# Block 1 of a two-model kernel: decay rows by DMA instead of by matmul, and a new order of slabs around the state scan

## The chip, the core and the metric

One core of one Trainium2 chip. The time is device microseconds of one execution of the whole program, median of several runs. The kernel before took 2516.99 us (three runs, 2516.38 to 2517.11).

## The reference, cut to what matters

The program runs two layers of block 1 and two of block 2 on one sequence of 512 positions with 1024 features. Only block 1 is changed. In it, one normed input `h` is multiplied by one wide matrix, and the columns feed three branches:

```python
h = rmsnorm(x, attn_norm_g[layer])
gm_u, gm_v, ssm_z, ssm_xbc, ssm_dt, da_q, da_k, da_v, gates = split_cols(h @ w_in[layer], IN_SIZES)
y_a = gelu(gm_u) * (causal(w_s) @ rmsnorm(gelu(gm_v)) + b_s)          # in chunks of 128
# mamba2: 16 heads of 64, 2 groups, state 128, chunks of 128
xs, bm, cm = split(silu(conv(xbc)));  dt = softplus(ssm_dt + bias)
a_cum = cumsum(dt * a)                                               # per head, per chunk
decay = exp(where(causal, a_cum[t] - a_cum[s], -inf))                # the head's decay matrix
y = (C.B * decay) @ (xs*dt) + C @ prev_state * exp(a_cum) + d*xs
y_b = rmsnorm(y * silu(z))
y_c = diff_attention(q, k, v)
merged = g0*(y_a @ w_branch_a) + g1*(y_b @ w_branch_b) + g2*(y_c @ w_branch_c)
```

For each head the decay needs `a_cum` as a row (position t along the free axis) on all 128 partitions; that row is what the change obtains in another way.

## The kernel before, in words

**Weights and precision.** All large products are made of three fp32r matmuls (high by high, low by high, high by low; `mm3`, L571 to L573). A weight slab is 128 x 1024 words (512 KB), for branches a and c 128 x 512 (256 KB). Each slab goes through four steps: SP issues its load (`load`, L545) as soon as the slab four places earlier is done; ACT rounds it to `w_hi` (L561, `hi_ahead`); DVE subtracts to get `w_lo` in place (L566, `lo_ahead`); PE multiplies. ACT and DVE work three slabs ahead of PE (`LEAD = 3`, `RAW = HI = 4`). A slab of 512 KB is 24 matmuls of 512 columns, one of 256 KB is 12.

**Queues.** Every engine runs one program written out by hand, in order. What is queued behind a waiting instruction waits too. PE writes slabs into four PSUM banks (`pg`, `take_bank`) and everything else into four more in rotation (`pm`, `take_pm`): the i-th use of `pm` waits until the use four before it has been emptied. The order of the `pm` uses is the list `PM.take(...)`.

**The stage in question**, once for each of the two layers (at 107 to 300 us and at 1020 to 1213 us in the profile). PE's order before: 12 xbc slabs; 4 z slabs; transposes of dt and cumulative decays (`dt_n`), then 4 z slabs with two transposes of xs (`xs_n`) ahead of each; 4 gu slabs, each followed by transposes of B or by a C.B product; the spatial mixing (`gm_mix`); 8 gate_a slabs with the three chunk states between them; 8 branch-a slabs, and between them for each pair of heads p two fp32r matmuls that spread a row of `a_cum` over all partitions (`ac_rows`, L2244, from a hi/lo split `ac_parts`) and the 28 small fp32 matmuls of the pair (`y_pair`, L2269 and L2272); then 12 qkv slabs. Each qkv group of four slabs fills four banks, tile tt after tile tt; bank tt is taken at the first slab of the group.

**Around the pairs**, for head h of pair p: DVE takes the minimum of row and column (`bounded`, L1535, reading the row in PSUM), ACT makes the exponentials (L1019 over 384 columns, L1021 four times 128), POOL multiplies the first by C (L2074), and DVE (even head, L1574) or POOL (odd head, L2077) multiplies the second by C.B. DVE adds the pair's result to `yf` (L1570), and merges each branch-a unit with its gate (L1566), which frees the unit's bank. POOL also makes `yf = d*xs` (L2049, 8 times, "y_init") and the low parts `ya_lo` (L555).

Of the kernel before, what the change touches and what calls it, by code (L numbers as in the profile page):

```python
# [13 lines left out]
P = 128  # L14
# [99 lines left out]
def program(nc, t, out, depth=DEPTH, depth2=DEPTH):  # L114
    with ExitStack() as ctx:
# [53 lines left out]
        head_row = sb("head_row", [P, SSM_H], F32R)  # L169
# [80 lines left out]
        wt_gm = conv_in[:, 0, 4:4 + SEQ].rearrange("p (g n) -> p g n", g=GM_G)  # L250
# [6 lines left out]
        xw = [conv_in[:, 2 + g, 4:4 + SSM_I // SSM_G] for g in range(SSM_G)]  # L257
# [8 lines left out]
        ac_parts = over("ac_parts", arena_at + 4 * 26624, [P, SEQ], F32R)  # L266
# [51 lines left out]
        for name, slabs, units in [("gv", 4, 4), ("dt", 0, 1), ("xbc", 12, 12), ("z", 8, 8), ("gu", 4, 4), ("gate_a", 8, 8), ("a", 8, 8), ("qkv", 12, 12),  # L318
                                   ("gate_b", 8, 8), ("b", 8, 8), ("gate_c", 8, 8), ("c", 8, 8), ("out", 8, 8), ("up", 44, 44), ("down", 24, 8)]:
# [7 lines left out]
        for p in range(PAIRS + 1):  # L327
            if p < PAIRS:
                PM.take(("ac_row", p), 2)
            if p >= 1:  # L330
                PM.take(("y", p - 1), 1)
# [157 lines left out]
        def gate_unit(i):  # L489
# [10 lines left out]
                "gm_vn": TT, "decay_in": 1, "decays": 1, "dt_ready": TT, "ac_split": 1, "gm_wt_ready": 1, "ya_ready": GM_G, "ya_hi_done": GM_G,  # L500
                "ya_split": GM_G, "ac_zeroed": 1, "cb_masked": SSM_G, "seg_bound": SSM_H, "seg_exp": SSM_H, "y_init": KD, "c_exp": SSM_H, "c_scaled": SSM_H, "decay_cb_even": PAIRS, "decay_cb_odd": PAIRS, "y_sq": KD, "y_sq_added": KD - 1, "xw_ready": SSM_G * (TT - 1), "y_gated": KD, "y_rms": 1, "y_inv": 1,
                "yb_ready": KD, "yb_hi_done": 8, "yb_split": 8, "qk_ssq": TT, "qk_rms": 1, "qk_ready": 1, "lam_dot": 1, "lam_exp": 1,
                "neg_max": 2 * DA_H * TT, "w_ready": DA_H * TT, "sub_summed": 1, "sub_rms": 1, "yt_ready": DA_H, "gates_b": 1, "gate_a_last": 1, "b_merged": KD, "gates_c": 1,
# [362 lines left out]
        def _(act):  # L866
# [24 lines left out]
            act.wait_ge(setup, 8)  # L891
# [22 lines left out]
            for l in range(depth):  # L914
# [65 lines left out]
                hi_ahead(SL["z"] + 2)  # L980
                z_in(0)
                for j in range(3, 7):
                    hi_ahead(SL["z"] + j)
                z_in(1)
                act.wait_ge(S("decay_in"), past("decay_in") + 1)
                nc.scalar.activation(dts[:, 128:256], dts[:, 128:256], ACT.Exp).then_inc(S("decays"), 1)
                hi_ahead(SL["z"] + 7)
                pm_filled(act, PM["gm_wt"])
                nc.scalar.activation(wt_gm.rearrange("p g n -> p (g n)"), pmb(PM["gm_wt"]), ACT.Copy).then_inc(pm_free[PM["gm_wt"] % 4], 1)

# [5 lines left out]
                for g in range(GM_G):  # L996
                    bank = unit_filled(act, SL["gu"] + g, UN["gu"] + g)
                    nc.scalar.activation(ya[:, g, :], bank, ACT.Gelu_apprx_tanh).then_inc(bank_free[(UN["gu"] + g) % BANKS], 1)
                    left_of("b_n" if g < 2 else "cb", bn if g < 2 else cb, g % 2)
                    hi_ahead(SL["gu"] + g)  # L1000
# [5 lines left out]
                act.wait_ge(S("y_init"), past("y_init") + KD)  # L1006
                for i in range(KD - 1):
                    gates(m_val, SL["gate_a"], UN["gate_a"], i, 1, ACT.Sigmoid)
                    hi_ahead(SL["gate_a"] + i)

                act.wait_ge(pm_ready, PM[("state", TT - 2)] + SSM_G)
                for p in range(PAIRS):
                    if p >= 2:
                        act.wait_ge(pm_ready, PM[("y", p - 2)] + 1)
                    for h in (2 * p, 2 * p + 1):
                        u = PM[("ac_row", p)] + h % 2
                        bank = pm_filled(act, u)
                        act.wait_ge(S("seg_bound"), past("seg_bound") + h + 1)
                        nc.scalar.activation(c_dec[h % 4], bank[:, P:SEQ], ACT.Exp).then_inc(S("c_exp"), 1)  # L1019
                        for c in range(TT):  # L1020
                            done = nc.scalar.activation(seg[:, h % 4, c, :], seg[:, h % 4, c, :], ACT.Exp, bias=acneg[:, c, h:h + 1])  # L1021
                            if c == 0:
                                done.then_inc(pm_free[u % 4], 1)
                        done.then_inc(S("seg_exp"), 1)
                    if p == 0:
                        gates(m_val, SL["gate_a"], UN["gate_a"], KD - 1, 1, ACT.Copy)
                        hi_ahead(SL["gate_a"] + KD - 1)
                    hi_ahead(SL["a"] + p)
                unit_left(act, UN["gate_a"] + KD - 1)
                nc.scalar.activation(m_val[:, KD - 1, :], m_val[:, KD - 1, :], ACT.Sigmoid).then_inc(S("gate_a_last"), 1)  # L1030

                hi_ahead(SL["qkv"])
                act.wait_ge(pm_ready, PM[("y", PAIRS - 1)] + 1)
# [4 lines left out]
                for c in (1, 2):  # L1038
                    hi_ahead(SL["qkv"] + c)
# [322 lines left out]
        def _(dve):  # L1362
# [11 lines left out]
            nc.vector.memset(head_row[:, :].bitcast(F32), 0.0).then_inc(setup, 1)  # L1374
# [32 lines left out]
            for l in range(depth):  # L1407
# [85 lines left out]
                lo_ahead(SL["z"])  # L1493
                lo_ahead(SL["z"] + 1)
                lo_ahead(SL["z"] + 2)
                u = PM["dt_n"]
                nc.vector.tensor_copy(dts[:, 0:128], pm_filled(dve, u)[:, 0:128]).then_inc(pm_free[u % 4], 1)
                dve.wait_ge(S("ac_zeroed"), past("ac_zeroed") + 1)
                chain(nc.vector.tensor_copy(ac_parts[0:SSM_H, :], ac_keep))
                nc.vector.tensor_tensor(ac_parts[32:32 + SSM_H, :], ac_keep, ac_parts[0:SSM_H, :].bitcast(F32), ALU.subtract).then_inc(S("ac_split"), 1)  # L1500
                lo_ahead(SL["z"] + 3)

                for c in range(TT):
# [5 lines left out]
                    if c == 0:  # L1509
# [1249 lines left out]
```

## Time and profile before

| what | value |
|---|---|
| median of three runs | 2516.99 us |
| span of the profiled execution | 2514.7 us |
| what lies around the span (difference to the median) | 2.3 us |
| busy share: PE, PE weight loads, DVE, ACT, POOL | 100%, 81%, 64%, 47%, 13% |
| TensorE clock granted in all 40 slices | full |
| DMA: mean share of 16 engines, mean rate | 35.7%, 88 GB/s |

The profile shows no time of its own for the whole of the profiled execution beside the span; the difference to the median of the runs stands for what lies around it. A busy PE in this profile is a chain of overlapping matmuls with modelled ends: the time of one matmul in a chain is read from start to start, not from its duration.

### The profile page before, as it was taken

What the parts mean: (1) busy time and instruction counts of PE and PEld (TensorE: products, weight loads), DVE (VectorE), ACT (ScalarE), POOL (GpSimd) and SP (SyncE); (2) the same over time, 40 slices, a digit from 0 to 9 for tenths busy, and PEclk for the clock granted to TensorE, in tenths of its full rate; (3) what the DMA queues carried; (4) which work ended last, traced back from release to release, by engine and by line L of the source; (5) the groups of instructions that cost most, each with busy time, mean ns of one, the idle gap of its engine ahead of it and who ended that gap; (6) DMA issues with size and microseconds to landing.
All of it is one profiled execution on the core that took longest, in us unless ns stands there. A gap on an engine that the chain in (4) does not pass through costs nothing.

```text
span 2514.7 us, 34027 instructions
## 1 busy us (share of the span) xinstructions
PE 2505.0 (100%) x12261; PEld 2048.5 (81%) x12261; DVE 1605.5 (64%) x2461; ACT 1186.3 (47%) x2185; POOL 317.8 (13%) x248
## 2 busy tenths in 40 slices
PE   9999999999999999999999999999999999999999
PEld 7887887888888887887877888888888777887777
DVE  6735767567777347538767567774355777647765
ACT  6534545544333235436354443333246555564563
POOL 1024201010111000225020101110020001210010
PEclk9999999999999999999999999999999999999999
DMA  6433342333333353452444333333324322332322
GB/s 143 95 83 66 87 92 75 65 112 93 100 92 98 97 112 88 88 80 71 92 81 69 96 92 100 92 99 96 99 79 108 86 62 62 91 93 76 84 59 76
DMA packets 400031, 221.94 MB, mean 88 GB/s; under 512 B 52736, under 2 KB 377376, under 8 KB 399648
## 3 DMA queue, kind: packets, MB, share of 16 engines
q1 hardware_dynamic: 399904, 220.26, 35.7%
q8 instruction: 79, 1.29, 0.2%
q14 instruction: 48, 0.39, 0.1%
HBM read 218.12 MB, written 2.10 MB: 88 GB/s over the span
## 4 chain that ended last, share of the span: by engine, by line
PE 96%; DVE 2%; ACT 1%; issue 1%; DMA 1%; SPq 0%; DVEq 0%
PE pg L571 29%; PE pg L572 28%; PE pg L573 28%; PE pm L671 3%; PE pm L2465 1%; PE pm L2349 1%; PE pm L2439 1%; PE pm L2314 1%; PE pm L2269 1%; DVE w_lo L566 1%; PE pm L2479 1%; PE pm L2506 1%; ACT w_hi L561 0%; PE pm L2272 0%; PE pm L2252 0%
## 5 line engine op out<-in xcount | busy, mean ns | idle before, releaser
L566 DVE TENSOR_TENSOR w_lo<-w_raw,w_hi 128x1024 fp32r<-128x1024 f32 (+3 forms) x440 | 538.8, 1226 | 516.3 <-ACT w_hi L561 514.4
L571 PE MATMUL pg<-h_hi,w_hi 128*128 128x512 f32 x1856 | 737.1, 397 | 0.3 <-ACT arena L1229 0.2
L573 PE MATMUL pg<-h_hi,w_lo 128*128 128x512 f32 x1856 | 723.3, 390 | 0.0
L572 PE MATMUL pg<-h_lo,w_hi 128*128 128x512 f32 x1856 | 723.1, 390 | 0.0
L561 ACT ACTIVATE w_hi<-w_raw 128x1024 fp32r<-128x1024 f32 (+3 forms) x440 | 434.1, 988 | 588.4 <-DMA w_raw<-in_w_in_dram 239.5
L571 PEld LDWEIGHTS pg<-h_hi,w_hi 128*128 128x128 f32 x1856 | 348.6, 188 | 77.6 <-issue 8.9
L573 PEld LDWEIGHTS pg<-h_hi,w_lo 128*128 128x128 f32 x1856 | 348.4, 188 | 73.4
L572 PEld LDWEIGHTS pg<-h_lo,w_hi 128*128 128x128 f32 x1856 | 348.9, 188 | 69.5 <-issue 1.4
L571 PE MATMUL pg<-w_hi,h_hi 128*128 128x512 f32 (+2 forms) x440 | 164.9, 375 | 0.0
L573 PE MATMUL pg<-w_hi,h_lo 128*128 128x512 f32 (+2 forms) x440 | 162.0, 368 | 0.0
L572 PE MATMUL pg<-w_lo,h_hi 128*128 128x512 f32 (+2 forms) x440 | 161.9, 368 | 0.0
L1743 DVE SCALAR_TENSOR_TENSOR arena<-conv_in,par,arena 128x512 f32<-128x512 f32 x176 | 131.9, 749 | 15.3 <-DVE arena L1743 11.0
L571 PE MATMUL pg<-f_hi,w_hi 128*128 128x512 f32 x352 | 136.9, 389 | 0.0
L572 PE MATMUL pg<-f_lo,w_hi 128*128 128x512 f32 x352 | 136.9, 389 | 0.0
L573 PE MATMUL pg<-f_hi,w_lo 128*128 128x512 f32 x352 | 136.9, 389 | 0.0
L1143 ACT ACTIVATE arena<-conv_in,par 128x512 f32<-128x512 f32 x88 | 71.9, 817 | 127.0 <-DVE conv_in L1737 127.0
L555 POOL TENSOR_TENSOR f_lo<-arena,f_hi x44 | 57.9, 1317 | 516.3 <-DVE f_hi L1751 516.3
L1737 DVE TENSOR_TENSOR conv_in<-pg,rinv 128x512 f32<-128x512 f32 x88 | 60.8, 691 | 80.7 <-PE pg L573 80.6
L571 PE MATMUL pg<-nb_parts,w_hi 128*128 128x512 f32 x256 | 101.9, 398 | 0.0
L573 PE MATMUL pg<-nb_parts,w_lo 128*128 128x512 f32 x256 | 99.7, 389 | 0.0
L571 PEld LDWEIGHTS pg<-w_hi,h_hi 128*128 128x128 f32 x440 | 82.8, 188 | 13.8 <-issue 1.9
L572 PEld LDWEIGHTS pg<-w_lo,h_hi 128*128 128x128 f32 x440 | 82.9, 188 | 12.9 <-issue 1.0
(417 smaller groups left out, 3753.2 us busy)
## 6 DMA issues: line engine op xcount, KB each, us to landing
w_raw<-in_w_in_dram SPq DMA_DIRECT2D x184, 512.0 KB, 4.7
w_raw<-in_ffn_w_up_dram SPq DMA_DIRECT2D x88, 512.0 KB, 3.7
w_raw<-in_w_out_dram SPq DMA_DIRECT2D x32, 512.0 KB, 3.6
w_raw<-in_ffn_w_down_dram SPq DMA_DIRECT2D x32, 512.0 KB, 3.6
w_raw<-in_w_branch_b_dram SPq DMA_DIRECT2D x16, 512.0 KB, 3.5
w_raw<-in_ffn_w_down_dram SPq DMA_DIRECT2D x16, 384.0 KB, 3.2
w_raw<-in_w_branch_a_dram SPq DMA_DIRECT2D x16, 256.0 KB, 2.9
w_raw<-in_w_branch_c_dram SPq DMA_DIRECT2D x16, 256.0 KB, 2.8
```

What stands on the lines that cost most here:

```text
L555: return nc.gpsimd.tensor_tensor(lo, value, hi.bitcast(F32), ALU.subtract)
L561: nc.scalar.activation(w_hi[:, s % HI, 0:n], w_raw[:, s % RAW, 0:n], ACT.Copy).then_inc(hi_done, 1)
L566: nc.vector.tensor_tensor(w_lo[:, s % RAW, 0:n], w_raw[:, s % RAW, 0:n], w_hi[:, s % HI, 0:n].bitcast(F32), ALU.subtract)\
L571: nc.tensor.matmul(dst, l_hi, r_hi, start=start, stop=False)
L572: nc.tensor.matmul(dst, l_hi, r_lo, start=False, stop=False)
L573: return nc.tensor.matmul(dst, l_lo, r_hi, start=False, stop=stop)
L671: done = nc.tensor.transpose(dst, src, ident[0:src.shape[0], 0:src.shape[0]])
L1143: nc.scalar.activation(facc[:, j, :], conv_in[:, j, 4:4 + SEQ], ACT.Identity, bias=fconv_b[:, bass.ds(i, 1)], scale=fconv_w[:, i, 2:3]).th ...
L1737: nc.vector.tensor_tensor(conv_in[:, j, 4:4 + SEQ], unit_filled(dve, SL["up"] + j, UN["up"] + j, 4, it), inv[:, :], ALU.mult)\
L1743: nc.vector.scalar_tensor_tensor(facc[:, j, :], conv_in[:, j, 4 - a:4 - a + SEQ], fconv_w[:, i, 2 - a:3 - a], facc[:, j, :], ALU.mult, ALU ...
L2269: done = nc.tensor.matmul(bank[rows, c * P:(c + 1) * P], xdt[:, c, h * 64:h * 64 + 64], seg[:, h % 4, c, :], start=True, stop=c == 0)
L2314: done = nc.tensor.matmul(bank[:, qi * P:(qi + 1) * P], wt(h, kt)[:, (qi - kt) * P:(qi - kt + 1) * P], qkv[:, kt, 1024 + h * P:1024 + (h + ...
```

## The change: what it does

1. **Rows.** The 32 `ac_rows` matmuls, the memset, cast and subtraction that split `a_cum`, and `head_row` go. SP stores `a_cum` once (16 x 512 words) in DRAM, and 16 broadcast DMAs a layer (256 KB each, 128 packets of 2 KB) bring one head's row to all partitions in SBUF. The first four land in the buffer of the result itself (`seg`), the others in `m_val[4..7]` and two spare places.
2. **Distance.** Rows, minimum and exponentials of pair p+2 are made while pair p is multiplied (before: p+1). Rows of pairs 0 and 1 are issued after z slab 4, of 2, 3, 5 after z slab 7, of 4 after gate_a slab 5, of 6 after gate_a slab 6, of 7 after branch-a slab 0.
3. **Order on PE.** `gm_wt` and the gu slabs come ahead of z, with the mixing after gu 1 and gu 2; `dt_n` after gu 3; all four B and C.B products between the two z halves; the states after z slabs 4, 5, 6; each `y_pair` after its gate_a slab; the 8 branch-a slabs run with nothing between them.
4. **Sigmoid of gate a.** Its copies go to SBUF first, and two calls over 2048 columns follow at the end of the gate_a slabs.
5. The other engines' programs follow this order; `xw` (POOL's weighted xs) moves from `conv_in` to the arena, `wt_gm` too.

The core of the diff:

```diff
+        ac_rows_dram = nc.dram_tensor("ac_rows", [DEPTH, SSM_H, SEQ], F32).ap()
-        for name, slabs, units in [..., ("xbc", 12, 12), ("z", 8, 8), ("gu", 4, 4), ("gate_a", 8, 8), ("a", 8, 8), ("qkv", 12, 12),
+        for name, slabs, units in [..., ("xbc", 12, 12), ("gu", 4, 4), ("z", 8, 8), ("gate_a", 8, 8), ("a", 8, 8), ("qkv", 12, 12),
-        for name, n in [("sums1", 1), ("spread1", 1), ("dt_n", 1), ("xs_n0", 2), ("ac_last", 1), ("xs_n", 6), ("gm_wt", 1), ("b_n", 2), ("cb", 2), ("gm_mix", 4)]:
+        for name, n in [("sums1", 1), ("spread1", 1), ("gm_wt", 1), ("gm_mix", 4), ("dt_n", 1), ("xs_n0", 2), ("ac_last", 1), ("xs_n", 6), ("b_n", 2), ("cb", 2)]:
 # ACT, gate_a stage
+                for i in range(KD):
+                    gates(m_val, SL["gate_a"], UN["gate_a"], i, 1, ACT.Copy)
+                    hi_ahead(SL["gate_a"] + i)
+                    if i + 2 < PAIRS:
+                        carried_exps(i + 2)          # waits for y_pair(i) and for the rows
+                        chunk_exps(i + 2)
+                for a in range(2):
+                    half = m_val[:, 4 * a:4 * a + 4, :]
+                    nc.scalar.activation(half, half, ACT.Sigmoid).then_inc(S("gates_a"), 1)
 # DVE, behind the gu slabs
+                u = PM["dt_n"]
+                nc.vector.tensor_copy(dts[:, 0:128], pm_filled(dve, u)[:, 0:128]).then_inc(pm_free[u % 4], 1)
+                lo_ahead(SL["gu"] + 3)
+                for g in range(GM_G):
+                    dve.wait_ge(S("ya_ready"), past("ya_ready") + g + 1)
+                    nc.vector.tensor_copy(ya_hi(g), ya[:, g, :]).then_inc(S("ya_hi_done"), 1)
 # then xs times dt (frees the banks of xs_n), one chunk at a time
 # DVE, gate_a stage
+                for p in range(PAIRS):
+                    u = PM[("y", p)]
+                    nc.vector.tensor_tensor(yf[:, p, :], yf[:, p, :], pm_filled(dve, u), ALU.add)...
+                    if p + 2 < PAIRS:
+                        bounded(p + 2)               # waits for the rows
+                    if p + 1 < PAIRS:
+                        even_decays(p + 1)
+                    lo_ahead(SL["gate_a"] + p, 0, 0)
 # DVE, branch-a stage
+                for i in range(KD):
+                    lo_ahead(SL["a"] + i, 0, 0)
+                    dve.wait_ge(S("gates_a"), past("gates_a") + i // 4 + 1)
+                    nc.vector.tensor_tensor(m_val[:, i, :], m_val[:, i, :], unit_filled(dve, SL["a"] + i, UN["a"] + i), ALU.mult)...
+                    if i >= 2:
+                        y_square(i - 1)
 # POOL: y_init waits for DVE's copy of dt_n
+                pool.wait_ge(S("xs_ready"), past("xs_ready") + 2)
+                pm_left(pool, PM["dt_n"])
                 for i in range(KD):
                     nc.gpsimd.tensor_scalar(yf[:, i, :], xb[:, i, :], d_skip[:, i:i + 1], None, ALU.mult).then_inc(S("y_init"), 1)
+                for g in range(GM_G):
+                    pool.wait_ge(S("ya_hi_done"), past("ya_hi_done") + g + 1)
+                    low_part(ya_lo[:, g, :], ya[:, g, :], ya_hi(g)).then_inc(S("ya_split"), 1)
 # PE, gate_a and branch-a stages
                 for p in range(PAIRS):
-                    if p >= 1:
-                        ac_rows(p)
-                    slab_t(pe, SL["a"] + p, UN["a"] + p, 0, 0, ya_hi, h_parts(ya_lo), 4)
-                    if p >= 1:
-                        y_pair(p - 1)
+                    slab_t(pe, SL["gate_a"] + p, UN["gate_a"] + p, 0, 0, hh, hl, KD)
+                    y_pair(p)
+                for i in range(KD):
+                    slab_t(pe, SL["a"] + i, UN["a"] + i, 0, 0, ya_hi, h_parts(ya_lo), 4)
 # SP
+                    for p in {5: (4,), 6: (6,), 8: (7,)}.get(i, ()):
+                        ac_rows(p)                   # two broadcast DMAs of 256 KB
```

## Rows read from the trace of the kernel before

**Rows 1.** The page: busy time by engine, and the chain by engine.
```profile
PE 2505.0 (100%) x12261; PEld 2048.5 (81%) x12261; DVE 1605.5 (64%) x2461; ACT 1186.3 (47%) x2185; POOL 317.8 (13%) x248
...
PE 96%; DVE 2%; ACT 1%; issue 1%; DMA 1%; SPq 0%; DVEq 0%
```
**Rows 2.** Timeline of PE around a pair (start us, us, engine, line, operation).
```profile
244.01 0.39 PE L573 MATMUL pg<-nb_parts,w_lo 128*128 128x512 f32 x1
244.33 0.66 PE L2269 MATMUL pm<-arena 128*64 128x128 f32 x8
...
245.69 0.39 PE L2272 MATMUL pm<-sq,arena 128*64 128x128 f32 x4
246.01 0.72 PE L2244 MATMUL pm<-ac_parts,head_row 128*128 128x512 f32 x2
246.57 0.39 PE L571 MATMUL pg<-nb_parts,w_hi 128*128 128x512 f32 x1
246.80 0.40 PE L572 MATMUL pg<-ya_lo,w_hi 128*128 128x512 f32 x1
```
**Rows 3.** Timeline of PE behind the last pair, which no row matmul follows.
```profile
276.01 0.50 PE L571 MATMUL pg<-w_hi,h_hi 128*128 128x512 f32 x1
276.35 0.39 PE L572 MATMUL pg<-w_lo,h_hi 128*128 128x512 f32 x1
```
**Rows 4.** Timeline of PE around the transposes of dt and xs.
```profile
128.76 0.39 PE L573 MATMUL pg<-h_hi,w_lo 128*128 128x512 f32 x1
129.08 0.41 PE L671 MATMUL pm<-c_pack,arena 16*128 16x16 f32 x4
...
130.61 0.33 PE L2215 MATMUL pm<-rinv,last_row 128*128 128x64 f32 x2
130.75 0.47 PE L571 MATMUL pg<-h_hi,w_hi 128*128 128x512 f32 x1
131.06 0.39 PE L572 MATMUL pg<-h_lo,w_hi 128*128 128x512 f32 x1
```
**Rows 5.** Timelines of PE and ACT at the end of gu slab 0.
```profile
161.00 0.39 PE L573 MATMUL pg<-h_hi,w_lo 128*128 128x512 f32 x1
...
161.43 0.60 ACT L998 ACTIVATE arena<-pg 128x512 f32<-128x512 f32 x1 [0.97 <-PE pg L573]
```
**Rows 6.** DVE's casts of ya by line (ns min/median/max), and POOL beside them.
```profile
L1530 DVE CAST nb_parts<-arena x4: 419/965/1518, 193.6 to 195.7; 128x512 fp32r<-128x512 f32 x4
...
194.13 5.53 POOL L555 TENSOR_TENSOR ya_lo<-arena,nb_parts 128x512 fp32r<-128x512 f32 x4 [3.02 <-DVE nb_parts L1530]
```
**Rows 7.** POOL's y_init by line, its running calls, and DVE beside them.
```profile
L2049 POOL TENSOR_SCALAR arena<-arena,par x8: 1564/1596/2586, 131.3 to 144.1; 128x512 f32<-128x512 f32 x8
...
141.04 4.82 POOL L2049 TENSOR_SCALAR arena<-arena,par 128x512 f32<-128x512 f32 x3
...
143.21 1.23 DVE L566 TENSOR_TENSOR w_lo<-w_raw,w_hi 128x1024 fp32r<-128x1024 f32 x1 [4.98 <-ACT w_hi L561]
```
**Rows 8.** DMA issues (KB each, us to landing): gate_c 5; gate_a 5; qkv 2, both layers.
```profile
w_raw<-in_w_in_dram SPq DMA_DIRECT2D x1, 512.0 KB, 11.5
...
w_raw<-in_w_in_dram SPq DMA_DIRECT2D x1, 512.0 KB, 14.2
...
w_raw<-in_w_in_dram SPq DMA_DIRECT2D x1, 512.0 KB, 4.8
...
w_raw<-in_w_in_dram SPq DMA_DIRECT2D x1, 512.0 KB, 5.1
```
**Rows 9.** DMA issues of the whole run: a broadcast of one row; the output matrix.
```profile
w_raw<-in_w_out_dram SPq DMA_DIRECT2D x32, 512.0 KB, 3.6
...
arena<-in_gm_b_s_dram SPq DMA_DIRECT2D x2, 256.0 KB, 5.3
```
**Rows 10.** Timelines of ACT and DVE: a slab's two splits, a merge.
```profile
99.57 1.06 ACT L561 ACTIVATE w_hi<-w_raw 128x1024 fp32r<-128x1024 f32 x1 [8.85 <-DMA w_raw<-in_w_in_dram]
...
248.41 0.68 DVE L1566 TENSOR_TENSOR arena<-arena,pg 128x512 f32<-128x512 f32 x1
249.61 1.47 DVE L1574 TENSOR_TENSOR arena<-arena 128x512 f32<-128x512 f32 x1
```

More of the change, by code:

```diff
@@ L326, in program @@
             PM.take(("state", c), SSM_G)
-        for p in range(PAIRS + 1):
-            if p < PAIRS:
-                PM.take(("ac_row", p), 2)
-            if p >= 1:
-                PM.take(("y", p - 1), 1)
+        for p in range(PAIRS):
+            PM.take(("y", p), 1)
         PM.take("y_sums", 1)
@@ L1004, in gates, with carried_exps @@
                         nc.scalar.activation(dst[:, i, :], unit_filled(act, s + i, u + i), func).then_inc(bank_free[(u + i) % BANKS], 1)
[L1006 to L1012, printed above, removed]
+                def carried_exps(p):
                     if p >= 2:
@@ L1028, in _ @@
[L1028 to L1033, printed above, removed]
-                for i in range(KD):
+                hi_ahead(SL["z"])
+                act.wait_ge(S("decay_in"), past("decay_in") + 1)
+                nc.scalar.activation(dts[:, 128:256], dts[:, 128:256], ACT.Exp).then_inc(S("decays"), 1)
@@ new lines, in _ @@
+                hi_ahead(SL["z"] + 1)
+                for p in range(2):
+                    carried_exps(p)
+                hi_ahead(SL["z"] + 2)
+                z_in(0)
+                hi_ahead(SL["z"] + 3)
+                for g in range(SSM_G):
+                    left_of("b_n", bn, g)
+                for g in range(SSM_G):
+                    left_of("cb", cb, g)
+                hi_ahead(SL["z"] + 4)
+                for p in range(2):
+                    chunk_exps(p)
+                    hi_ahead(SL["z"] + 5 + p)
@@ L1527, in _ @@
-                lo_ahead(SL["gate_a"], 0, 0)
-                for g in range(GM_G):
-                    dve.wait_ge(S("ya_ready"), past("ya_ready") + g + 1)
-                    nc.vector.tensor_copy(ya_hi(g), ya[:, g, :]).then_inc(S("ya_hi_done"), 1)
-                def bounded(p):
-                    for h in (2 * p, 2 * p + 1):
-                        bank = pm_filled(dve, PM[("ac_row", p)] + h % 2)
-                        nc.vector.tensor_tensor(seg[:, h % 4], by_chunk(bank), acn[:, :, h:h + 1].broadcast_to([P, TT, P]), ALU.min).then_inc(S("seg_bound"), 1)
@@ L1583, in _, with y_square @@
+                def y_square(i):
                     dve.wait_ge(S("y_sq"), past("y_sq") + i + 1)
@@ new lines, in _ @@
+                for g in range(SSM_G):
+                    bank = take_pm(pe, PM["cb"] + g)
+                    for c in range(TT):
+                        cs = slice(c * P, (c + 1) * P)
+                        done = nc.tensor.matmul(bank[:, cs], xb[:, 8 + g, cs], xb[:, 10 + g, cs], start=True, stop=True)
+                    done.then_inc(pm_ready, 1)
+                for j in range(4):
+                    slab_n(pe, SL["z"] + 4, UN["z"] + 4, hh, hl, 512, 4, 2, j, features=True)
+                    if j < TT - 1:
+                        pe.wait_ge(S("xw_ready"), past("xw_ready") + SSM_G * (j + 1))
```

351 lines of the change are left out of this document (180 added, 171 removed).

## The prediction

> **What bounds the kernel now.** I read the page's busy table and its chain first, then the timeline of PE through the changed stage, then the lines and landings of whatever hands PE its data. The table has PE busy all the time, and the chain is PE for 96% [rows 1]: nothing else ends last anywhere for long. The timeline of PE says the same more sharply. In a run of slab matmuls one starts every 0.227 us, and I found no wait in the stage from 42 to 500 us: pairs, transposes and slabs stand end to end. So the stage is bound by the work that PE gets. Work that is taken off PE is won in full. But the covers are now at zero idle, so any new wait of PE is lost in full too. The question is only what the new order makes late. The profile's span is 2514.7 us and the median of the runs 2.3 us more; I work on the span's rows and add the result to the median, 2517.0.
>
> **Removed from PE: 7.6 us.** A pair with its row matmuls: from their start at 246.01 to the second matmul of the next slab at 246.80 is 0.79 us [rows 2]. The pair with none behind it: 276.01 to 276.35, 0.34 us [rows 3]. The two row matmuls cost 0.45 us, and there are 8 pairs in 2 layers: 16 x 0.45 = 7.2 us. Changing between slab matmuls and the small fp32 ones costs too: going in 0.32 instead of 0.23 us, coming out 0.31 instead of 0.23 [rows 4], near 0.2 us a group. By the two programs there are 21 such groups a layer before and 20 after: 0.4 us more. What SP, DVE and POOL shed or add (memset, cast, subtraction; 16 row DMAs) is not on PE's path by itself.
>
> **Added: PE waits for DVE's copy of dt_n, 0.5 us.** The last-row product must wait until DVE has copied dt_n. Counted from the end of gu slab 3, PE gets to it after 0.09 + 1.53 = 1.62 us [rows 4]. DVE is now queued behind the product of ya with the mixing, and that behind ACT's gelu of the same slab: 0.20 us until ACT sees the slab, 0.60 for gelu [rows 5], 0.68 for the product, 0.29 for the copy, some 0.1 of semaphores, less 0.08 of overlap: 1.8 to 1.9 us. So 0.25 us a layer. Bounds 0 and 0.4.
>
> **Added: DVE's casts beside POOL's y_init, 4.8 us.** DVE's copy of dt_n releases POOL's 8 calls of y_init (1.56 us each if nothing holds them, [rows 7]). DVE goes on with a low part (1.23 us), which POOL's first call waits for (its longest took 2.59), then with the four casts of ya, and only then with xs times dt, which empties the banks of the transposes. Before, the casts stood elsewhere, and POOL was at ya_lo: the free casts took 0.42 us and the two beside POOL 1.5 us each, POOL's four calls taking 5.53 us together, so that both engines advanced one call every 1.45 us [rows 6]. If y_init holds a cast in the same way, the casts end at 1.85 + 1.23 + 1.56 + 0.3 + 3 x 1.45 = 9.3 us and the first product with dt at 10.0. PE is through z slab 0 at 2.0 + 5.44 = 7.45, transposes one bank (0.44), and needs for the next the bank of xs_n 0, at 7.9: it waits 2.1 us. With y_init's own pace (1.56 + 0.14) it is 2.8. Lower end: a low part that began 0.6 us into a y_init call was not held (1.23 us, [rows 7]); if the casts aren't either, they end before 5 us and the wait is nothing. I take the casts' own row, as the nearer one, and 2.4 us a layer between its pace and y_init's: 4.8. Ends 0 and 5.6.
> The Trainium skill's page "SBUF — State Buffer", section "SBUF: two separate sides", says that DVE in a two-port mode, or with two SBUF inputs, and GpSimd hold the shared port pair exclusively for a whole instruction. The casts' row agrees. The low part beside y_init doesn't (it should have waited 0.95 us); there the trace decides, and it is why I don't take this term as certain. By the rule the term would be its upper end.
>
> **Added: branch a into qkv, 2.9 us.** Let T be the end of gate_a slab 7. The pair after it takes 1.68 + 0.2 us [rows 2], a branch-a slab 12 x 0.227 = 2.72, and nothing lies between them now (before, a pair and its rows: 5.07 us from slab to slab). qkv slab 2 can be loaded when branch-a slab 6 is done, at T + 20.9. It then takes 0.2 to issue, 4.8 us to land in layer 0 and 5.1 in layer 1 [rows 8], 1.06 for the high part, 1.23 for the low part [rows 10, 7], which DVE has queued ahead of the last merge, and 0.68 for that merge [rows 10]: T + 29.0 and 29.3. The merge frees the bank that qkv slab 0 takes for its fourth tile, at T + 1.9 + 8 x 2.72 + 3 x 1.36 = 27.7. PE waits 1.3 and 1.6 us. If such a load lands like the output matrix (3.6, [rows 9]) it is 0.1 each; if the four qkv loads, now 2.72 us apart instead of 5.07, delay each other by a microsecond it is about 2.5 each. Ends 0.2 and 5.
>
> **Added: rows of pair 4 behind gate_a slab 5, 2.5 us.** Let U be the end of gate_a slab 1. SP then issues the load of gate_a 5, and behind it the rows of pair 4. The load of index 5 is slow in every set of gates: 14.2 us for gate_a 5 in layer 1, and 11.5 for gate_c 5 in layer 0, which went out only after its predecessor had landed [rows 8]. The rows can hardly land before it. DVE waits for them in `bounded(4)`, and queued behind that is the even product of pair 3, which PE needs one slab later. A period is now 24 x 0.227 + 1.9 = 7.35 us, so pair 3 starts at U + 14.7; less two minima (1.27), the product (0.68) and 0.15 of hand-over, the rows must have landed by U + 12.6. In layer 0 they land at 0.2 + 11.5 and a little, some 12.7: 0.2 us of wait. In layer 1 at 14.4 to 15.5: 2.3 us. Ends 0 (transfers that pass each other) and 7 (each row adding 1.3 us).
> The Trainium skill, "DMA: Bandwidth & Descriptors", "Queues, rings and completion order", says that a DMA's semaphore write lands only after every earlier write of that DMA engine. No row here shows two such transfers in question; by that rule the lower end is excluded.
>
> **What I cost at nothing.** In the gate_a stage ACT has per period a copy (0.6), a split (1.06), two exponentials of 384 and eight of 128 (3.5): 5.2 of 7.35 us. DVE has 4.9 and POOL 3.3. DVE's minimum now reads the row in SBUF, beside POOL's calls, where reading PSUM was never held; a DVE product beside POOL took 1.47 instead of 0.68 us [rows 10]. Two such delays still leave the even product about 0.4 us before PE asks for it. The states are one slab apart instead of two: POOL's two products (2.1 us) have 5.4. The two long sigmoids and a table load (5.1 us) end at T + 6.4, and branch-a slab 3 is wanted at T + 10. Rows of pairs 0 to 3 and 5 have 10 us or more. If this cover fails it is by slow rows (below).
>
> **Sum.** -7.6 + 0.5 + 4.8 + 2.9 + 2.5 = +3.1: 2517.0 + 3.1 = 2520.1 us.
>
> **Rivals.**
> (a) The casts aren't held by y_init. For it: the low part that wasn't. Against: every cast beside another POOL call was. Then -7.6 + 0.5 + 2.9 + 2.5 = -1.7: 2515.3.
> (b) The order holds and only the shorter PE work shows: rows pass the slow load, the casts are free, the hand-over to qkv costs 0 to 2.9. For it: no wait stands anywhere in the stage before, at smaller distances. Time: 2509.5 to 2512.3, faster.
> (c) Slow rows, the case well beyond the slower side. 128 packets read the same 2 KB. The broadcast of gm_b, alike in form, took 5.3 us [rows 9]. If a row holds the queue for 2.5 us instead of about 1, the rows of pairs 0 and 1 delay the emptying of banks ahead of the C.B products (0.5 us a layer), and pair 3 waits 1.4 us longer in each layer, pair 6 in the second by 2.6 (its rows stand behind gate_a 6). That is 1 + 2.8 + 2.6 = 6.4 more: 2526.5. It decides once rows land more than 12.6 us after U.
> (d) The change doesn't do what it says, if PE finds the rows' successors late everywhere and the distance of two pairs isn't reached; I see no sign of it, as all engines have more than 2 us of slack per period.
>
> **How the numbers follow.** All three waits (forecast): 0.42, 2517 to 2524. (a) 0.25, 2513 to 2518. (b) 0.16. (c) 0.17. A measurement of this kernel tells 0.2%, 5 us, from no change: faster is below 2512.0, which is nearly all of (b) and a little of (a), 0.18; slower is above 2522.0, (c) and a quarter to a third of the forecast's own case, 0.30; the same 0.52. The range leaves out the fastest part of (b) and the end of (c): 2511 to 2526.5.
>
> **What would show it.** Timeline of PE after: no L2244; in each layer a wait of about 2 us at the fourth xs transpose behind z slab 0, released by DVE; a wait of 0 to 3 us ahead of pair 3, with DVE's minimum of pair 4 released by a row's DMA; a wait above 1 us at the fourth tile of qkv slab 0, released by the last merge. DVE's casts of ya at 1.5 us or more. The prediction is wrong if casts take 0.42 us beside y_init, if the rows of pair 4 land under 12 us, or if another wait above 1 us stands in the stage.

## The result: 9.6 us slower, and the profile after

The changed kernel takes 2526.41 us (median of 5 runs, 2524.68 to 2527.85) against 2516.82 us for the kernel before beside it: ratio 1.0039, 95% interval 1.0028 to 1.005. The forecast was 2520.1, range 2511.0 to 2526.5. The sign was right, the size a third of what came; the time stands 0.1 us inside the upper end of the range. The profiled execution's span is 2523.5 us, 8.8 more than before. Timed again beside the last experiments, the changed kernel took 2526.64. Its executions differ more than those of the kernel before (2524.7 to 2529.8 in the ten), and the two profiled ones show a reason: the granted clock of TensorE fell once in the stage in the first and three times in the second, each time at a cost of 1.3 to 2.5 us.

The page after, busy time and chain, answers to [rows 1]. PE does 32 matmuls less, and the chain is now PE for 94% instead of 96%; of the other shares only DMA's has grown in whole per cent, from 1 to 2.

```profile
PE 2501.9 (99%) x12229; PEld 2043.9 (81%) x12229; DVE 1624.3 (64%) x2454; ACT 1198.4 (47%) x2191; POOL 322.5 (13%) x246
...
PE 94%; DVE 2%; DMA 2%; issue 1%; ACT 1%; SPq 0%; DVEq 0%
```

I measured the changed stage in PE's timeline from the start of the last dt matmul to the first transpose behind the qkv slabs. Before: 314.9 us in each layer (41.70 to 356.63 and 953.94 to 1268.87). After: 317.4 in layer 0 (41.10 to 358.51) and 320.4 in layer 1 (957.09 to 1277.52). The stretch ahead of layer 0's stage is 0.6 shorter, the one between the two 1.3 longer, the rest of the program 0.1 longer: 2.5 + 5.5 - 0.6 + 1.3 + 0.1 = 8.8.

**Ahead of pair 3.** The timeline of PE in layer 0 and then layer 1 (start us, us, engine, line, operation). From 217.09 to 219.33 and from 1132.12 to 1136.24 no matmul starts: waits of 2.01 and 3.89 us beyond the 0.227 of slab matmuls. The step into a pair is 0.32 even without a wait, so pair 3 comes 1.92 and 3.80 us late, 9.28 and 11.16 us after pair 2 instead of 7.36. In layer 1 the pair then runs at half pace: 1136.24 to 1139.42 is 3.18 us, where layer 0 has 1.68.

```profile
217.09 0.39 PE L570 MATMUL pg<-h_hi,w_lo 128*128 128x512 f32 x1
219.33 0.66 PE L2308 MATMUL pm<-arena 128*64 128x128 f32 x8 [1.85 <-issue]
...
221.01 0.50 PE L568 MATMUL pg<-h_hi,w_hi 128*128 128x512 f32 x1
...
1132.12 0.39 PE L570 MATMUL pg<-h_hi,w_lo 128*128 128x512 f32 x1
1136.24 1.12 PE L2308 MATMUL pm<-arena 128*64 128x128 f32 x8 [3.73 <-issue]
...
1139.42 0.80 PE L568 MATMUL pg<-h_hi,w_hi 128*128 128x512 f32 x1
```

PE's row names "issue". DVE's rows show what it was: the minimum of pair 4 starts when a row's DMA lands, and the even product of pair 3, queued behind, ends 0.1 us before PE goes on.

```profile
216.50 1.32 DVE L1549 TENSOR_TENSOR arena<-arena,rinv 128x512 f32<-128x512 f32 x2 [3.96 <-DMA arena<-ac_rows]
217.74 1.49 DVE L1555 TENSOR_TENSOR arena<-arena 128x512 f32<-128x512 f32 x1
...
1133.44 1.30 DVE L1549 TENSOR_TENSOR arena<-arena,rinv 128x512 f32<-128x512 f32 x2 [5.87 <-DMA arena<-ac_rows]
1134.65 1.48 DVE L1555 TENSOR_TENSOR arena<-arena 128x512 f32<-128x512 f32 x1
```

The DMA issues there (KB, us to landing): gate_a slab 5 and the rows behind it, in layer 0 and in layer 1.

```profile
w_raw<-in_w_in_dram SPq DMA_DIRECT2D x1, 512.0 KB, 12.7
arena<-ac_rows SPq DMA_DIRECT2D x1, 256.0 KB, 13.2
...
w_raw<-in_w_in_dram SPq DMA_DIRECT2D x1, 512.0 KB, 14.6
arena<-ac_rows SPq DMA_DIRECT2D x2, 256.0 KB, 15.1
```

**The clock behind it.** Stretches of layer 1 (us, busy time of PE, its weight loads, DVE, ACT, POOL, granted clock, DMA share, GB/s). After the wait the granted clock is 0.50, the lower of TensorE's two levels (1.2 GHz), until about 1142.

```profile
1132.00:1136.00 4.00, 0.51 (x3) 0.09 (x1) 2.56 (x3) 3.54 (x9) 1.90 (x2) 0.85 0.96 240
1136.00:1139.00 3.00, 2.76 (x26) 2.79 (x28) 3.00 (x3) 1.39 (x5) 3.00 (x2) 0.50 0.73 160
1139.00:1142.00 3.00, 3.00 (x13) 2.17 (x10) 3.00 (x5) 1.62 (x3) 0.27 (x2) 0.56 0.39 114
1142.00:1146.00 4.00, 4.00 (x19) 3.13 (x17) 3.54 (x3) 2.61 (x9) 4.00 (x3) 1.00 0.03 8
```

From the start of pair 3 to that of pair 4 it is 9.89 us; an undisturbed period is 7.36. The fall costs 2.5 us.

**Branch a into qkv.** PE, DVE and ACT in layer 0. PE waits twice for a merge (L1611), 0.58 and 2.12 us. Each merge stands behind a low part (L563), that behind a high part (L558), and that behind a load. The four loads of the group took 5.0, 5.4, 6.3 and 6.5 us in layer 0; it is the third that ends the longer wait.

```profile
274.86 0.39 PE L570 MATMUL pg<-w_hi,h_lo 128*128 128x512 f32 x1
275.66 0.50 PE L568 MATMUL pg<-w_hi,h_hi 128*128 128x512 f32 x1 [0.41 <-DVE arena L1611]
...
276.92 0.39 PE L570 MATMUL pg<-w_hi,h_lo 128*128 128x512 f32 x1
279.26 0.50 PE L568 MATMUL pg<-w_hi,h_hi 128*128 128x512 f32 x1 [1.96 <-DVE arena L1611]
...
277.39 1.23 DVE L563 TENSOR_TENSOR w_lo<-w_raw,w_hi 128x1024 fp32r<-128x1024 f32 x1 [1.18 <-ACT w_hi L558]
278.53 0.68 DVE L1611 TENSOR_TENSOR arena<-arena,pg 128x512 f32<-128x512 f32 x1
...
276.30 1.06 ACT L558 ACTIVATE w_hi<-w_raw 128x1024 fp32r<-128x1024 f32 x1 [2.03 <-DMA w_raw<-in_w_in_dram]
```

**The casts.** DVE and POOL behind the gu slabs, to be compared with [rows 6, 7]. The four casts take 2.25 us together (0.42, 0.83, 0.42, 0.82 one by one), beside y_init: the first three lie wholly within its first call, which ends at 138.29. The first product with dt starts at 138.50. PE waits nowhere at the transposes behind z slab 0.

```profile
135.18 1.22 DVE L563 TENSOR_TENSOR w_lo<-w_raw,w_hi 128x1024 fp32r<-128x1024 f32 x1
136.33 2.25 DVE L1541 CAST nb_parts<-arena 128x512 fp32r<-128x512 f32 x4
138.50 1.27 DVE L1563 TENSOR_TENSOR arena<-pm,rinv 128x512 f32<-128x512 f32 x2
...
135.39 7.85 POOL L2080 TENSOR_SCALAR arena<-arena,par 128x512 f32<-128x512 f32 x4 [18.48 <-DVE rinv L1537]
```

**Smaller ones.** PE waits 0.87 us ahead of gu slab 0 in layer 0: the bank is emptied by the second reading of ACT's first tap, which ACT starts only after it has split gu slab 1, whose load landed late. (PE's row names DVE's low part L563 as what ended the wait, as that ends at the same time; in run 8 PE starts gu slab 0 while that low part is still going, so it was the bank.)

```profile
105.57 1.06 ACT L558 ACTIVATE w_hi<-w_raw 128x1024 fp32r<-128x1024 f32 x1 [2.02 <-DMA w_raw<-in_w_in_dram]
106.54 0.76 ACT L892 ACTIVATE arena<-pg,par 128x512 f32<-128x512 f32 x1
107.20 0.59 ACT L893 ACTIVATE conv_in<-pg 128x512 f32<-128x512 f32 x1
```

PE waits 0.23 us in each layer ahead of the last-row product. At 933 us it waits 1.17 us for a bank that DVE frees behind the low part of a gv slab, whose load landed late.

### The profile page after: what moved, and what is told of

The parts are those of the page before. It is cut to its first block, busy times and chain, and to the rows that moved or that the text cites. A ratio compares the mean times of both kernels' runs of the same rounds, so it can differ in the third digit from the quotient of the medians.

```text
span 2523.5 us, 33840 instructions
## 1 busy us (share of the span) xinstructions
PE 2501.9 (99%) x12229; PEld 2043.9 (81%) x12229; DVE 1624.3 (64%) x2454; ACT 1198.4 (47%) x2191; POOL 322.5 (13%) x246
## 4 chain that ended last, share of the span: by engine, by line
PE 94%; DVE 2%; DMA 2%; issue 1%; ACT 1%; SPq 0%; DVEq 0%
PE pg L568 28%; PE pg L570 28%; PE pg L569 28%; PE pm L687 3%; DMA w_raw<-in_w_in_dram 1%; PE pm L2501 1%; PE pm L2385 1%; PE pm L2475 1%; PE pm L2350 1%; PE pm L2308 1%; DVE w_lo L563 1%; ACT w_hi L558 1%; PE pm L2515 1%; PE pm L2542 1%; PE pm L2311 0%
## 5 line engine op out<-in xcount | busy, mean ns | idle before, releaser
L563 DVE TENSOR_TENSOR w_lo<-w_raw,w_hi 128x1024 fp32r<-128x1024 f32 (+3 forms) x440 | 545.4, 1241 | 475.7 <-ACT w_hi L558 473.9
L558 ACT ACTIVATE w_hi<-w_raw 128x1024 fp32r<-128x1024 f32 (+3 forms) x440 | 434.1, 988 | 631.9 <-DMA w_raw<-in_w_in_dram 278.6
```

Source lines behind the costliest of these rows:

```text
L558: nc.scalar.activation(w_hi[:, s % HI, 0:n], w_raw[:, s % RAW, 0:n], ACT.Copy).then_inc(hi_done, 1)
L563: nc.vector.tensor_tensor(w_lo[:, s % RAW, 0:n], w_raw[:, s % RAW, 0:n], w_hi[:, s % HI, 0:n].bitcast(F32), ALU.subtract)\
```

## The experiments

All were timed beside the kernel before; ratios are to it. That kernel took 2516.3 us beside runs 1 to 4, 2515.9 beside 5 to 8 and 2516.5 beside 9 to 12, so half a microsecond between runs of different groups says nothing. My theory behind the result: PE lost what it gained to three waits, ahead of pair 3 with the half clock behind it, at the hand-over to qkv, and small ones. Rivals: rows that are slow in themselves; DVE held by POOL; an order with no slack left, so that waits only move.

**1. Rows of pair 4 ahead of the slow load.**

```diff
-                    for p in {5: (4,), 6: (6,), 8: (7,)}.get(i, ()):
+                    for p in {4: (4,), 6: (6,), 8: (7,)}.get(i, ()):
```

> The rows of pair 4 are issued ahead of the load of gate_a slab 5 instead of behind it; nothing else differs from the changed kernel (2526.4 us). Theory (the rows are held behind a slow load): the rows land some 5 us after their issue, DVE's minimum of pair 4 is early, PE's waits ahead of pair 3 (2.0 us in layer 0, 3.9 in layer 1) go, and with the long one the stretch at half clock behind it (3.4 us): -9.3, about 2517.1 us. Rival 1 (a broadcast row is slow in itself, wherever it stands): the rows still take 12 us or more, counted from an issue a few us earlier, and 2 to 4 us of wait stay: 2520 to 2524. Rival 2 (the even product is held by POOL's calls, not by the rows): the product still ends about 1.5 us late in each layer: about 2521.

Measured: 2519.2 us (2517.8 to 2521.8), ratio 1.0012, interval 1.0003 to 1.0021. Pair 3 starts 7.36 us after pair 2 in both layers, and the half clock behind it is gone. 2.1 us of the expected 9.3 didn't come. The expectation had priced the half clock at 3.4 us, where the trace has 2.5; in layer 1 a new wait of 0.43 us stands ahead of pair 4 (see run 3); and in the profiled execution the clock fell behind the hand-over wait of layer 0 (1.6 us), which in the changed kernel's first one it had not.

**2. Merges ahead of low parts.**

```diff
                 for i in range(KD):
-                    lo_ahead(SL["a"] + i, 0, 0)
+                    if i < 5:
+                        lo_ahead(SL["a"] + i, 0, 0)
                     ... merge(i)
+                    if i >= 5:
+                        lo_ahead(SL["a"] + i, 0, 0)
```

> In the branch-a stage DVE's merges 5, 6 and 7 stand ahead of the low parts of qkv slabs 0, 1 and 2 instead of behind them; the rest is the changed kernel. Theory (banks come free late because the merges are queued behind low parts that wait for loads): PE's waits at the third and fourth tile of qkv slab 0 (0.58 + 2.12 us in layer 0, 0.56 + 1.68 in layer 1) go: -4.9, about 2521.5 us; the waits ahead of pair 3 and the half clock behind the second stay. Rival (the loads of the qkv slabs themselves are what PE lacks): the wait only moves to the start of qkv slab 2 or 3, and the time is 2525 to 2526.5.

Measured: 2518.9 us (2516.5 to 2520.7), ratio 1.0009, interval 1.0000 to 1.0018. No wait is left at qkv slab 0, nor did one appear at slabs 1 to 3: the loads were early enough. The gain is 7.5 and not 4.9. Behind each of the four waits one more step was 0.11 us longer, 0.4 in all. And in five of the eight other profiles that have the hand-over wait (run 12's among them), the clock fell behind it in layer 0, at a cost of 1.2 to 1.6 us; that explains part. About a microsecond stays open.

**3. Both.**

> Both edits: rows of pair 4 ahead of the slow load, merges 5 to 7 ahead of the low parts. Theory: the savings add, -9.3 and -4.9: about 2512.2 us, which is faster than the kernel before by 4.6 us; what is left of the difference to the 7.6 us taken off PE is 0.9 us at gu slab 0, 0.5 at the last-row product and 1.2 at the start of layer 1. Rival (the order without those waits meets the next one, because every engine's slack of a period was used already): they don't add, 2515 or more.

Measured: 2512.3 us (2511.5 to 2514.2), ratio 0.9985, interval 0.9976 to 0.9994: 14.1 us less than the changed kernel, where 14.2 was expected. What is left shows in ACT's and DVE's timelines in layer 1. The load of gate_a slab 5 landed after 15.3 us, as slow as ever. ACT splits that slab ahead of the exponentials of pair 4, and DVE makes its low part ahead of all that follows; PE waits for pair 4's even product, 1.84 us. The exponentials end at 1131.92, 2.6 us before DVE comes to that product, so what ends last is DVE's own queue behind the low part. The minimum and the product shown took 1.78 and 1.48 us while POOL was at work, where one alone takes 0.68.

```profile
1127.69 1.06 ACT L558 ACTIVATE w_hi<-w_raw 128x1024 fp32r<-128x1024 f32 x1 [7.39 <-DMA w_raw<-in_w_in_dram]
...
1129.48 2.44 ACT L1030 ACTIVATE arena<-arena,rinv 128x128 f32<-128x128 f32 x8
...
1128.78 1.23 DVE L563 TENSOR_TENSOR w_lo<-w_raw,w_hi 128x1024 fp32r<-128x1024 f32 x1 [4.89 <-ACT w_hi L558]
...
1132.78 1.78 DVE L1549 TENSOR_TENSOR arena<-rms,rinv 128x512 f32<-128x512 f32 x1
1134.48 1.48 DVE L1555 TENSOR_TENSOR arena<-arena 128x512 f32<-128x512 f32 x1
...
1136.06 0.66 PE L2311 MATMUL pm<-arena 128*64 128x128 f32 x8 [1.68 <-DVE arena L1555]
```

**4. PE kept busy, a little.** `nc.tensor.transpose(bank[:, 0:P], ident, ident)` 16 times ahead of pair 3's waits.

> Sixteen transposes of the identity (1.8 us of PE, no use made of them) stand ahead of the waits of pair 3 in the changed kernel. Theory (the clock fell because PE stood still for 3.9 us): the wait in layer 0 is 0.2 us and in layer 1 2.1 us instead of 2.0 and 3.9, PE's own end of both is where it was, the granted clock stays at 1.0 behind them as it does behind the 2.0 us wait of layer 0, and 3.4 us are won though PE has more to do: about 2523 us. Rival 1 (the fall has another cause, such as the load of the engine before it): the time stays at 2526.4. Rival 2 (the rows are not what PE waits for): the transposes come on top, 2528 or more.

Measured: 2524.85 us (2523.4 to 2525.9), ratio 1.0032, interval 1.0020 to 1.0045. Inconclusive: layer 1's wait was still 2.95 us behind the transposes, and the clock fell again. Hence run 10.

**5 and 8. The waits taken out, and the matmuls put back.**

```diff
# 8: run 3, and
+                    if i != 2:                        # ACT: split of gate_a slab 5 ...
                         hi_ahead(SL["gate_a"] + i)
                     if i + 2 < PAIRS:
                         carried_exps(i + 2)
                         chunk_exps(i + 2)
+                    if i == 2:                        # ... behind the exponentials of pair 4
+                        hi_ahead(SL["gate_a"] + i)
...
+                    if p == 3:                        # DVE: its low part behind the even product of pair 4
+                        lo_ahead(SL["gate_a"] + 2, 0, 0)
# and ACT's split of gu slab 1 behind two taps
# 5: run 8, and ahead of each pair
+                    for _ in range(2):
+                        nc.tensor.matmul(bank, hh(0)[:, 0:P], hh(0), start=True, stop=True)
```

> Rows of pair 4 ahead of the slow load and merges 5 to 7 ahead of the low parts, as in the third experiment (2512.3 us); besides, the high part of gate_a slab 5 stands behind ACT's exponentials of pair 4, its low part behind DVE's even product of pair 4, and the high part of gu slab 1 behind two of ACT's first taps. Theory (with the rows early, the slow load of gate_a slab 5 is late by another way: ACT splits it ahead of the exponentials of pair 4, and PE waits 0.3 us in layer 0 and 1.8 in layer 1 ahead of pair 4; and gu slab 0 waits 0.5 us for a bank that ACT empties behind the split of gu slab 1): 2.6 us go, 2509.7 us. Rival (the split is now late for gate_a slab 5 itself): the wait moves there, 2511.5 to 2513.

> The kernel of the next run (waits taken out), with two matmuls of 512 columns put ahead of each of the 16 pairs, into the bank that the pair overwrites; they read the normed input and nothing uses them. Theory (the matmuls for the rows were PE's time in full, 0.45 us a pair): 16 x 0.45 = +7.2 us over the next run, about 2517.1, which is the kernel before. Rival (the stage is no longer bound by PE everywhere, so that part of them disappears in waits): +2 to +5 us.

Measured: run 8 takes 2509.73 us (2508.9 to 2510.3), ratio 0.9975, interval 0.9965 to 0.9985, 6.2 us faster than the kernel before and the fastest of all. Run 5 takes 2517.18 us (2516.5 to 2517.7), ratio 1.0005, interval 0.9996 to 1.0014: +7.45 us. In the trace of run 8 every one of the 14 distances from pair to pair is 7.36 us, in run 5 every one is 7.81. The 0.45 us a pair are settled. Run 8 moves ACT's split and DVE's low part together, so it doesn't tell which of the two moves took run 3's wait away. Its stage takes 311.6 us in each layer against 314.9: 3.35 less, and with the 0.23 of the last-row wait 3.6, which is 8 x 0.45. Nothing is left for the 0.4 us of group changes.

**6. y_init with two tensor inputs.**

```diff
-  nc.gpsimd.tensor_scalar(yf[:, i, :], xb[:, i, :], d_skip[:, i:i + 1], None, ALU.mult)
+  nc.gpsimd.tensor_tensor(yf[:, i, :], xb[:, i, :], d_skip[:, i:i + 1].broadcast_to([P, SEQ]), ALU.mult)
```

> POOL's y_init calls become a product of two tensors (the skip weights broadcast) instead of a tensor with a column; all else is the changed kernel (2526.4 us). Theory (DVE's casts took 0.42 and 0.83 us beside y_init because that call reads one tensor; a POOL call that reads two holds the casts): casts of 1.4 us or more, the first product with dt some 2 to 3 us later, and PE waits about 2.4 us in each layer at the fourth xs transpose behind z slab 0, as the prediction had it: about 2531. Rival (the casts were never in the way of any POOL call, and what held them in the kernel before was something else): casts as in the changed kernel, no wait, 2526.4.

Measured: 2527.2 us (2525.6 to 2529.4), ratio 1.0046, interval 1.0032 to 1.0060. The mechanism is there, the price isn't. The four casts take 4.81 us instead of 2.25 (1.26 each, one per POOL call), and the first product with dt starts 4.73 us after the first cast instead of 2.17. But the POOL calls take only 1.22 us beside them, not 1.45, so PE waits 0.27 and 0.20 us and not 2.4 in each layer. The edit changes the number of tensors read and POOL's operation (TENSOR_SCALAR to TENSOR_TENSOR) at once; which of the two makes the hold, it doesn't tell.

```profile
134.44 1.23 DVE L563 TENSOR_TENSOR w_lo<-w_raw,w_hi 128x1024 fp32r<-128x1024 f32 x1
135.58 4.81 DVE L1541 CAST nb_parts<-arena 128x512 fp32r<-128x512 f32 x4
140.31 1.28 DVE L1563 TENSOR_TENSOR arena<-pm,rinv 128x512 f32<-128x512 f32 x2
...
134.61 7.67 POOL L2080 TENSOR_TENSOR arena<-arena,par 128x512 f32<-128x512 f32 x6 [18.44 <-DVE rinv L1537]
```

**7. Same moment, other place in the queue.** Rows of pair 4 ahead of the load of gate_a slab 5, and behind the wait for slab 1.

```diff
+                    if i == 4:
+                        wait(sp, slab_done, SL["gate_a"] + 2)
                     for p in {4: (4,), 6: (6,), 8: (7,)}.get(i, ()):
```

> The rows of pair 4 are issued at the same moment as in the changed kernel (when gate_a slab 1 is done), but in the queue ahead of the load of gate_a slab 5 instead of behind it. Theory (position in the queue, not time): they land 4 to 6 us after their issue, as rows elsewhere do, PE waits for nothing ahead of pair 3: within a microsecond of the first experiment, 2519. Rival (what counts is that they share the DMA engines with the slow load): they still land after 10 us or more, and the time is 2524 to 2526.5.

Measured: 2521.5 us (2518.8 to 2522.7), ratio 1.0022, interval 1.0013 to 1.0031. The rows land in 3 to 4 us though they are issued as late as in the changed kernel, and pair 3 doesn't wait. The load lands as late as ever. Layer 0, then layer 1:

```profile
arena<-ac_rows SPq DMA_DIRECT2D x2, 256.0 KB, 3.6
w_raw<-in_w_in_dram SPq DMA_DIRECT2D x1, 512.0 KB, 12.5
...
arena<-ac_rows SPq DMA_DIRECT2D x2, 256.0 KB, 3.3
w_raw<-in_w_in_dram SPq DMA_DIRECT2D x1, 512.0 KB, 15.7
```

Behind the rows, the load goes out about 1 us later in layer 1, so pair 4 there waits 2.23 us for its even product by the way of run 3, and the clock falls behind it. That is why the time is 2.3 us above run 1.

**9. Rows of pair 4 in a queue of their own.** ACT issues them (`nc.scalar.dma_start`) behind its copy of gate_a slab 1, SP no longer.

> The rows of pair 4 go through ACT's queue instead of SP's: ACT issues them behind its copy of gate_a slab 1, some 0.8 us after SP issued the load of gate_a slab 5. All else is the changed kernel (2526.4 us). Theory A (what holds the rows is their place behind the load in one queue): from a queue of their own they land 3 to 6 us after their issue, and the wait ahead of pair 3 goes, as in the run with the rows ahead of the load at the same moment: 2520 to 2522. Theory B (the DMA engines finish what they took first, whatever the queue): they land after 11 us or more, with the load, and the time is 2526 or, as ACT's issuing costs it a microsecond, a little more.

Measured: 2523.8 us (2521.6 to 2524.4), ratio 1.0027, interval 1.0016 to 1.0039. Neither theory whole. Issues of layer 0: the load, the first row, the second row.

```profile
w_raw<-in_w_in_dram SPq DMA_DIRECT2D x1, 512.0 KB, 13.9
arena<-ac_rows ACTq DMA_DIRECT2D x1, 256.0 KB, 7.6
...
arena<-ac_rows ACTq DMA_DIRECT2D x1, 256.0 KB, 14.2
```

The first row was issued at the same time as the load (202.51 and 202.50 us) and lands 6.3 us ahead of it; the second, issued 0.4 us later, lands 0.7 us behind the load. Layer 1 is alike: 9.2 and 16.5 us for the rows, 16.3 for the load. So a second queue gets a share of the DMA engines and no more: 7.6 and 9.2 us for a first row that took 3.1 us in run 7, where nothing slow stood ahead. PE still waits 1.49 and 3.82 us ahead of pair 3. The Trainium skill, "DMA: Bandwidth & Descriptors", "Queues, rings and completion order", says that each DMA engine takes turns between the queues it has work for; the first row's passing agrees.

**10. PE kept busy to the end of the wait.** 44 transposes, layer 1 alone.

> Forty-four transposes of the identity (4.7 us of PE, unused) stand ahead of the waits of pair 3, in layer 1 alone. Theory (TensorE's clock falls when PE stands still for 2.2 us or more): they fill the wait of 3.9 us, the clock stays at its upper level behind it, and pair 3 to pair 4 takes 7.36 us from start to start, where it took 9.89 us in the changed kernel; with 0.8 us of surplus transposes the net is -1.7 us: 2524.7. Rival (the fall has to do with the data or the DMA traffic of that moment): from pair 3 to pair 4 still some 9.9 us less nothing, and the time is 2527.

Measured: 2525.55 us (2522.5 to 2527.0), ratio 1.0035, interval 1.0021 to 1.0049; the median can't tell 0.9 us, the trace can. Layer 1, the stretches of the half clock above: granted 1.00 throughout, at a DMA share of 0.74 in the mean of the ten microseconds, where the changed kernel had 0.72.

```profile
1132.00:1136.00 4.00, 4.00 (x25) 3.44 (x25) 0.06 (x1) 1.06 (x1) 0.00 (x0) 1.00 0.71 197
1136.00:1139.00 3.00, 3.00 (x30) 3.00 (x28) 3.00 (x4) 2.98 (x9) 2.40 (x2) 1.00 0.87 196
1139.00:1142.00 3.00, 3.00 (x38) 2.56 (x37) 3.00 (x2) 0.89 (x3) 2.72 (x2) 1.00 0.65 147
```

From pair 2 to pair 4 it is 19.55 us; in the changed kernel 21.05. In layer 0 of the same run, with no transposes, PE waited 3.10 us and the next period was 8.76.

**11. Other columns for the slow load.** Gate 5 of branch a is computed with the weights of gate 1.

```diff
-                    w, c = (w_in, C_GATE + P * i) if i < KD else ...
+                    w, c = (w_in, C_GATE + P * (1 if i == 5 else i)) if i < KD else ...
```

> The load of gate_a slab 5 reads the columns of slab 1 instead of its own (gate 5 of branch a is computed with the wrong weights; sizes, order and places are the same). Theory A (the slow landing belongs to the columns that slab 5 reads): it lands in 6 to 9 us instead of 12.7 and 14.6, the rows of pair 4 with it, and both waits ahead of pair 3 and the half clock go: -7 to -8, about 2518.5. Theory B (it belongs to the moment: the rows and loads that are in flight there): it lands as before and the time stays at 2526.4.

Measured: 2517.2 us (2516.1 to 2520.5), ratio 1.0006, interval 0.9996 to 1.0015: -9.3 us against the changed kernel. Layer 0, then layer 1:

```profile
w_raw<-in_w_in_dram SPq DMA_DIRECT2D x1, 512.0 KB, 7.6
arena<-ac_rows SPq DMA_DIRECT2D x1, 256.0 KB, 7.7
...
w_raw<-in_w_in_dram SPq DMA_DIRECT2D x1, 512.0 KB, 8.9
arena<-ac_rows SPq DMA_DIRECT2D x2, 256.0 KB, 9.2
```

All 14 distances from pair to pair are 7.36. The slow landing belongs to the columns read, not to the moment. Nor is it that the other columns had been read before: on their first reading, four slabs earlier, they took 6.8 and 8.0 us. The run also prices the two waits with the clock behind the second: 9.3 us, where the trace of the changed kernel has 8.3.

**12. The changed kernel once more.**

> The changed kernel once more, as a control beside the other runs of this call: 2526.4 us by its first timing; the sums of the experiments are right if it is within 1.5 us of that.

Measured: 2526.64 us (2524.8 to 2529.8), ratio 1.0044, interval 1.0030 to 1.0058.

## Why the prediction was off

| step | forecast, us | found, us | from |
|---|---|---|---|
| row matmuls | -7.2 | -7.2 | run 5: +7.45; periods 7.81 and 7.36 |
| changes between groups | -0.4 | 0 | run 8's stage |
| last-row product | +0.5 | +0.5 | 0.23 + 0.23 |
| casts beside y_init | +4.8 | 0 | casts of 0.42 and 0.83 |
| branch a into qkv | +2.9 | +5.4 | 0.58 + 2.12 + 0.56 + 1.68, and 0.11 behind each |
| rows of pair 4 | +2.5 | +5.7 | 1.92 + 3.80 |
| clock behind it | not seen | +2.5 | 9.89 - 7.36 |
| gu slab 0; a gv slab; ahead of the stage | not seen | +0.9; +1.2; -0.6 | trace of after |

The column "found" sums to +8.4 of the span's 8.8; the rest is in excesses below 0.2 us. Without the term for the casts the forecast would have been -1.7 us, rival (a)'s: that the sign came out right is luck, as it rests on a term that was nothing while the others were too small.

**Removed work, last-row product: right.** The gain of the row matmuls was real and in full (the 0.4 us of group changes weren't found); all of the loss is in waits and in the clock behind them.

**"DVE's casts beside POOL's y_init": the step that failed.** It put 4.8 us where the runs show none: it took the price of casts beside `ya_lo` [rows 6] for casts beside y_init. Those POOL calls read two tensors, y_init reads one and a column. Run 6 makes y_init read two and use their operation, and the casts go from 2.25 to 4.81 us. The low part that was not held [rows 7] was the row to believe; rival (a) had the casts right. And even held, they cost PE 0.3 us a layer or less: the last one ended 4.7 us behind the low part, where the sum had 6.2 (1.56 + 0.3 + 3 x 1.45), as POOL's pace beside them was 1.2 us and not 1.45, and the first cast took 1.26 us and not 1.86. The rule of the Trainium skill, "SBUF — State Buffer", "SBUF: two separate sides", of a pair held for a whole instruction, agrees with run 6, where a cast ends once per POOL call. It doesn't agree with the changed kernel, where three casts of 0.42 and 0.83 us ran to their end within one y_init call; the measurement decides.

**"Rows of pair 4 behind gate_a slab 5": right in mechanism, mis-sized.** The rows landed 13.8 and 15.7 us after the end of gate_a slab 1 (forecast 12.7 and 14.4 to 15.5), and the even product took 1.49 us beside POOL, not 0.68. Those two give the waits within 0.1 us: 13.8 - 12.6 + 0.8 = 2.0 and 15.7 - 12.6 + 0.8 = 3.9. The product's share of it is worked out and was not tested by itself. I had the row for the product beside POOL [rows 10] and used it only where it was harmless. Experiments 1, 7 and 11 each take the wait away in another way. The clock behind a long wait was not in the sum at all: 2.5 us. Rival (c) ended at 2526.5, where the time came out, and its sign (rows later than 12.6 us) came too. But it had rows that are slow in themselves, and they are not (3 to 4 us in run 7); the agreement is luck.

**"Branch a into qkv": right in mechanism, too small.** The case that I named as about 2.5 us each came (2.9 and 2.5). The third of the loads, now 2.72 us apart, took 6.3 us instead of 4.8 and was split only at 276.30, and the merge before it had the same trouble on a smaller scale.

**Rival (b)** is what run 8 shows: without those waits the change is worth 6.2 us. Rival (d) is out: pairs do run two ahead.

## What to carry to other kernels

Where PE has no idle time, taking work off it pays in full only if every load, split and merge behind it still has slack at the shorter period. List each engine's queue with its slowest load in it, not its median one. A small DMA that others wait for goes ahead of a big load in the queue; a queue of its own is no substitute. And a wait of PE above 2 us should be priced with the slower clock that may follow.

## What the runs showed of the hardware

- The granted clock fell to 0.5 behind 10 of the 11 waits of PE ahead of a pair that lasted 2.18 us or more (one of 2.48 us passed), and behind none of those up to 2.01 us. It cost 1.3 to 2.8 us each time, and filling the wait with transposes kept it up. Length alone doesn't decide: at the hand-over of layer 0 it fell behind waits of 2.09 to 2.40 us in five runs, and not behind 2.97, 2.60, 2.12 and 2.03 us in four.
- A load of 512 KB in 512-byte pieces took 12.5 to 16.3 us for one set of columns, and 7.6 to 8.9 at the same moment for another, which had taken 6.8 and 8.0 when it was first read. Why those columns are slow, no run shows.
- The start of layer 1 has a wait of 0.3 to 1.2 us behind a gv load in every changed variant and none in the kernel before, in code that the change doesn't touch. In the changed kernel the first three of these loads took 9.5, 9.1 and 6.1 us, before 8.7, 7.2 and 4.7; why stays open.
